# Fewer row dot products inside tile 0's routing, more under the gates, and the gate exponentials ten expert blocks earlier

## The reference

```python
def peer_ffn(h, w_q, sub_k1, sub_k2, expert_u, expert_v):
    q = (ht @ w_q).reshape(T, PEER_HEADS, PEER_QDIM)
    s1 = jnp.einsum('thd,nd->thn', q[..., :PEER_HALF], sub_k1)
    s2 = jnp.einsum('thd,nd->thn', q[..., PEER_HALF:], sub_k2)
    v1, i1 = lax.top_k(s1, PEER_TOPK)
    v2, i2 = lax.top_k(s2, PEER_TOPK)
    cand = v1[..., :, None] + v2[..., None, :]
    vals, pos = lax.top_k(cand.reshape(...), PEER_TOPK)
    experts = jnp.take_along_axis(cand_idx, pos, axis=-1)
    gates = jax.nn.softmax(vals, axis=-1)
    a = jnp.einsum('cd,chkd->chk', xc, expert_u[experts])
    w = jax.nn.gelu(a) * gates
    return jnp.einsum('chk,chkd->cd', w, expert_v[experts])
```

## Time and profile before

| what | value |
|---|---|
| median of 3 runs | 1914.27 us (1913.71 to 1916.34) |
| the profiled execution, its own time | 1914.9 us |
| its span | 1912.9 us |
| mean granted TensorE clock | 0.992 |
| TensorE matmul busy | 1858.3 us, 97% |
| VectorE busy | 790.1 us, 41% |
| ScalarE, GpSimd busy | 259.0 us, 259.7 us |
| chain that ended last | TensorE 78%, DMA 9%, issue 6%, VectorE 5% |
| of it, fetches of v rows, of u rows | 6%, 3% |
| row fetches | 90 u rows and 90 v rows, median 9.2 and 10.0 us from issue to landing |

### The profile page before, as it was taken

How to read it: one execution, slowest core, us unless ns; L and a number is a source line. 1 busy time by engine, 2 the same in 40 slices (tenths; PEclk the granted TensorE clock), 3 DMA queues, 4 the chain that set the end, 5 groups by cost and what they waited for, 6 DMA issues and landing times.

```text
span 1912.9 us, 26633 instructions
## 1 busy us (share of the span) xinstructions
PE 1858.3 (97%) x10710; PEld 1530.9 (80%) x10710; DVE 790.1 (41%) x1739; ACT 259.0 (14%) x601; POOL 259.7 (14%) x252
## 2 busy tenths in 40 slices
PE   7999999999997999999999999999999999999996
PEld 6478575689997999999999957687786968687783
DVE  1410223248795877788644333231123113321122
ACT  1013333013443111000000011110000001110010
POOL 0100000000435333333433100000000000000000
PEclk9999999999998999999999999999999999999998
DMA  6434243244999999899999943364444435344441
GB/s 244 176 132 178 109 148 139 99 165 151 360 408 379 354 345 345 322 362 353 372 417 416 363 163 115 139 222 151 150 152 169 158 110 174 129 160 154 154 152 47
DMA packets 71138, 422.62 MB, mean 221 GB/s; under 512 B 8048, under 2 KB 8048, under 8 KB 31872
## 3 DMA queue, kind: packets, MB, share of 16 engines
q1 hardware_dynamic: 42048, 306.20, 43.6%
q0 software_dynamic: 28272, 111.74, 15.3%
q10 hardware_dynamic: 720, 3.27, 0.4%
HBM read 415.88 MB, written 5.24 MB: 220 GB/s over the span
## 4 chain that ended last, share of the span: by engine, by line
PE 78%; DMA 9%; issue 6%; DVE 5%; ACT 1%; POOL 0%; POOLq 0%; DVEq 0%; ACTq 0%
PE ps L409 23%; PE ps L449 10%; PE ps L752 9%; PE ps L478 7%; PE ps L760 7%; DMA arena<-v_rows,sparse_pairs 6%; PE ps L958 5%; PE ps L418 5%; PE ps L650 3%; DMA arena<-u_rows,sparse_pairs 3%; DVE arena L1555 1%; PE ps L684 1%; PE ps L773 1%; PE ps L546 1%; PE ps L914 1%
## 5 line engine op out<-in xcount | busy, mean ns | idle before, releaser
L409 PE MATMUL ps<-xT,ring 128*128 128x256 f32 x1920 | 420.6, 381 | 2.6 <-DVE xT L1723 2.6
L409 PEld LDWEIGHTS ps<-xT,ring 128*128 128x128 f32 x1920 | 365.7, 191 | 58.2 <-issue 7.0
L752 PE MATMUL ps<-xT,ring 128*128 128x168 f32 x2048 | 299.7, 309 | 0.2 <-ACT arena L1149 0.2
L760 PE MATMUL ps<-arena,ring 128*128 128x168 f32 (+1 forms) x2048 | 297.2, 307 | 0.0
L752 PEld LDWEIGHTS ps<-xT,ring 128*128 128x128 f32 x2048 | 294.5, 192 | 0.5 <-issue 0.5
L760 PEld LDWEIGHTS ps<-arena,ring 128*128 128x128 f32 x2048 | 292.3, 190 | 0.5 <-issue 0.5
L449 PE MATMUL ps<-ring,arena 128*128 128x512 f32 x448 | 196.9, 597 | 3.2 <-DVE arena L1899 2.8
L478 PEld LDWEIGHTS ps<-xT,ring 128*128 128x128 f32 x1536 | 173.4, 192 | 3.0 <-issue 2.9
L478 PE MATMUL ps<-xT,ring 128*128 128x128 f32 x1536 | 174.1, 275 | 0.0
L449 PEld LDWEIGHTS ps<-ring,arena 128*128 128x128 f32 x448 | 84.7, 192 | 104.0 <-issue 99.5
L1917 POOL TENSOR_SCALAR stat<-stat 128x1 f32<-128x1 f32 (+2 forms) x23 | 4.4, 190 | 1016.6 <-DVE stat L1798 759.5
(11 more groups left out here) (245 smaller groups left out, 1394.5 us busy)
## 6 DMA issues: line engine op xcount, KB each, us to landing
ring<-stream SPq DMA_DIRECT2D x292, 1024.0 KB, 5.1
arena<-second_params POOLq DMA_DIRECT2D x6, 1024.0 KB, 5.4
kv_scratch<-arena POOLq DMA_DIRECT2D x4, 1024.0 KB, 8.2
arena<-kv_scratch POOLq DMA_DIRECT2D x2, 2048.0 KB, 11.2
arena<-second_params POOLq DMA_DIRECT2D x1, 1536.0 KB, 6.6
arena<-u_rows,sparse_pairs POOLq DMA_INDIRECT x90, 9.2
arena<-v_rows,sparse_pairs POOLq DMA_INDIRECT x90, 10.0
arena<-mem_T ACTq DMA_DIRECT2D x1, 1024.0 KB, 7.8
```

Of the source, the lines that this page charges most:

```text
L409: ins = pe.matmul(ps[:, bank, t * T:(t + 1) * T], w[:, k * 2 * P + t * P:k * 2 * P + (t + 1) * P], act[:, k, :], start=(k == 0), stop=(k = ...
L752: ins = pe.matmul(ps[:, o % 2, 0:DENSE], w[:, (o % 2) * D + k * P:(o % 2) * D + (k + 1) * P], xT[:, k, 0:DENSE], start=(k == 0), stop=(k = ...
L760: ins = pe.matmul(ps[:, 4 + k // 2, c:c + DENSE], w[:, (o % 2) * D + k * P:(o % 2) * D + (k + 1) * P], H[:, n, :], start=False, stop=last, ...
```

## The change

Five numbers of the hand-written order change. Nothing is computed differently.

- Inside tile 0's routing VectorE does 18 row dots and not 36 (one behind each step of `best16` and not two, and the number at the end of the routing lowered).
- Between the end of the routing and the selector copies it does 16 (18 to 34) and not 10 (36 to 46).
- Under the first half of the gates it does 46 (34 to 80) and not 38 (46 to 84), and the fetch order follows, since U_FIRST is also GpSimd's.
- Under the second half of the gates it does 44 row adds in 21 groups and not 42; so 20 adds, 10 dots and 26 adds are left for the end, 56 in all, where it was 22, 6 and 26, 54 in all.
- ScalarE does the exponentials of tile 0 behind pair 21 (block 42) and not behind pair 26 (block 52).

```diff
@@ -46,10 +46,10 @@
-DOTS_ROUTING = 36
-DOTS_FIRST = 46
+DOTS_ROUTING = 18
+DOTS_FIRST = 34
 ROWS = 5
-U_FIRST = 84
+U_FIRST = 80
@@ -1150,7 +1150,7 @@
-            for i, stop in enumerate((2, 26)):
+            for i, stop in enumerate((2, 21)):
                 with act.Fori(at, stop) as n:
@@ -1610,9 +1610,9 @@
-                    best16(range(16), sc[:, i], top_v, ti, 2)
+                    best16(range(16), sc[:, i], top_v, ti, 1)
                     candidates(range(PH))
-                    best16(range(PH), cand, val, pu, 2)
+                    best16(range(PH), cand, val, pu, 1)
                     shift_gates()
                     pick(i, 0, PH, 2)
                     row_dots(DOTS_ROUTING - dots_done[0])
@@ -1710,7 +1710,7 @@
                     else:
-                        row_adds(2)
+                        row_adds(44 * (g + 1) // GROUPS - adds_done[0])
```

## The result

| what | before | with the change |
|---|---|---|
| median of 5 runs | 1916.34 us (1913.71 to 1918.15) | 1904.73 us (1902.06 to 1907.57) |
| ratio | | 0.9934, 95% interval 0.9922 to 0.9947 |
| profiled execution, span | 1912.9 us | 1900.1 us (its own time 1902.06) |
| mean granted clock | 0.992 | 0.995 |

The change makes the kernel 0.66% faster, 11.6 us in the medians and 12.8 us between the two profiled spans. The predicted 1904.0 us lies 0.7 us from the median. In part that is luck: it was worked out against a median of 1914.27 us, and the kernel before had 1916.34 us beside the changed one; of the 11.6 us won, 10.3 were predicted. In a second series of five runs the changed kernel had 1904.51 us, ratio 0.9940 (0.9926 to 0.9953).

A forecast was written before the change was run, and what follows sets the result against it. TensorE, busy 97% of the span, was taken as the bound, with the row line 4.1 us behind at the fold. Terms: 9.97 + 1.88 - 1.5 = 10.3 us off 1914.27, giving 1904.0 us; range 1901.8 to 1909.6.

The forecast's parts named there:

- The first gap goes: Before tile 0's routing transposes: routing ends at 561.2, 28 us before TensorE asks, so 9.97 us of idle time go.
- The low clock behind it: Blocks 56 to 63, behind the gap: 128 records take 18.45 us and not 20.33, 1.88 us won.
- The exponentials cost nothing: ScalarE, block 42: the exponential and table loads fit into an existing wait for TensorE; `shift_gates` has 16 us of cover.
- The selector copies: L1665, after block 63: done at about 605, needed at 608.8; no cost, cover of 2 to 4 us.
- Under the gates: TensorE's 7.39 us groups: two or three dots or adds fit, 8.3 us of lateness is hidden; no cost on TensorE.
- The end of the row line: Before the fold: 56 rows from 922.5 to 1076.0, TensorE done at 1074.5, so about 1.5 us of waiting given back.
- The sum: Whole kernel: 9.97 + 1.88 - 1.5 = 10.3 us won, so 1904.0 us against 1914.27.
- the upper end of the range: Last 51 rows at 2.9 us instead of 2.81: fold 4.3 us later; with 1.3 us of spread, 1909.6.
- TensorE alone: Rival at the fold: rows come slightly faster, the fold waits for nothing, full 11.85 us won, 1902.4; chance 0.25.
- the first two cases: At the fold: the forecast itself, waiting about 1.5 us for rows (0.62), or no wait and 1902.4 us (0.25).
- the row line could become the bound: Rival at the fold: row line ends at 1087.8, fold waits 13.3 us, 1915.8 or 1917.7; chance 0.04.
- The rival of late copies: Rival after block 63: rows at 4.1 us each, copies done at 627.7, 18.9 us late, 1923.3; chance 0.03.

The follow-up runs named there:

- The run without them: Changed kernel with tile 0's exponentials put back behind pair 26: 1917.05 us, ratio 1.0004.
- The two kernels with 6 dots: Kernel before with DOTS_ROUTING 30, DOTS_FIRST 40: exponentials behind pair 26, 1903.16 us, ratio 0.9929; behind pair 21, 1904.40 us, ratio 0.9941.
- the one-hots' run: Changed kernel with U_FIRST 84, 48 adds, and first one-hots built without waiting for block 63's gelu: 1901.25 us, ratio 0.9919.
- the run with late copies: Changed kernel with DOTS_FIRST 46, so 28 dots and not 16 before the selector copies: 1926.14 us in a single execution.
- the kernel with the rows earlier: Changed kernel with U_FIRST 84 and 48 adds under the gates, 48 rows left for the end: 1903.14 us, ratio 0.9938.
- the kernel with both waits shortened: Changed kernel with U_FIRST 84, 48 adds, one-hots not waiting for block 63's gelu, L409 waiting for single sums: 1902.24 us, again 1898.65 us.

## Why the prediction was right, point by point

- **The first gap goes: right.** 9.97 us are gone. I had L1640 done at 561.2 and tile 0's exponential as what sets it. It starts at 560.64 and ends at 560.93. VectorE waited 1.2 us for the exponential (L1620) there. The margin of 28 us is measured too.
- **The low clock behind it: right, slightly small.** The 128 matmuls take 18.3 to 18.5 us. But I had left the transposes at the 1.12 us that the last four took at the low clock; all eight now take 1.04. TensorE gained 12.6 us until the fold and not 11.85, and this is most of the difference: L792 up to block 56 took 11.69 us and takes 1.04, which is 10.65 and not 9.97.
- **The exponentials cost nothing: right**, and I had underrated them. I treated them as a condition for the gap alone. The run without them shows that their second use is larger: the 16 dots before the copies cannot start earlier than they end, and only the five buffers fill meanwhile.
- **The selector copies: right.** They start at 604.49 and end at 605.4, as expected, 2.5 us before TensorE needs them. But the reason that I gave for 605, some five rows fetched before, did not hold: the first of the 16 dots had its row at hand, the second waited 2.5 us for its own, and they came 2.8 us apart in the mean (560.85 to 603.34). With five at hand the copies would have been done near 599 (an estimate: 561.2 + 5 x 1.145 + 11 x 2.81 + 0.9), so the 605 was partly luck, and 607.1, my bound without them, was reasoned better. The two kernels with 6 dots, late by 1.6 and 4.2 us, lie beyond this edge. It is the nearest cliff of the changed kernel.
- **Under the gates: right.** No new wait of TensorE; the 46 dots and 44 adds are hidden. The two groups with a third add are longer than I had them: an add takes 1.39 us from start to start (five in 6.83 us), so such a group takes 3.69 + 3 x 1.39 = 7.9 us of VectorE and not 7.5. The cover hides that too.
- **The end of the row line: right in kind.** I had it from 922.5 to 1076.0 and a wait of 1.5 us. It ran from 921.58 to 1074.18, and the wait is 0.46 us, 0.41 in the second series. The pace was 2.81 us as before (52 steps from 926.89 to 1072.90). The start came 0.9 us earlier than I had it, mostly for the same 0.7 us of transposes, and the 56 rows took 152.6 us and not 153.5.
- **The sum:** 9.97 + 1.88 - 1.5 = 10.3 against 12.0 us measured at L409. The medians, 11.6 us apart, lie between. (In the upper end of the range, 51 rows at 0.09 us more are 4.6 us and not 4.3.)
- **The rivals.** TensorE alone did not quite end it: the wait of 0.46 us says which of the first two cases it was. The time alone does not, and 11.6 us lie nearer to that rival's 11.85 than to the 10.3 of the forecast. That the row line could become the bound was right as a mechanism; its price was too simple. Ten more rows cost 20 us of waiting and not 28, and the low clock behind a long wait cost 3.3 us in the fold alone, where I had 1.9 for all of it. The rival of late copies was priced at 4.1 us a row; with 28 dots it gave 21 us of wait at a mean of 2.4 us a row (561.1 to 628.2).

What is left open is small for the change itself: 1.1 us of the one-hots' run, and why the executions with six dots and late exponentials differ by up to 10 us, which no single profile places.

## What to carry to other kernels

When work is moved out of the way of one wait, look for the next point at which the same engine is waited for, and for everything that the engine itself waits for in between; here the eighteen dots and the exponentials were worth nothing apart and 12 us together. Move only as much as ends the wait with a margin that you can name: with six dots the time could not be told from that with eighteen, though the copies were then late. A second stream that is just behind the bounding engine, like the rows here, caps what that engine can gain, and its end should be costed with the same care as the gap.

## What the runs showed of the hardware

- A stream that shares the DMA engines speeds up by itself when its neighbour stops: rows came every 2.8 us beside the weight stream and every 1.5 us once TensorE had stood for about 8 us and the stream waited for its ring (the run with late copies: 408 GB/s at 616 to 618 us, 215 at 620 to 622). Some of them had landed by then, and VectorE took those at its own pace.
- The low clock behind a wait costs very different amounts. Behind the 20.5 us wait the fold took 7.02 us and not 3.75. Behind the wait of 2.58 us before L409, the same in all of these kernels, the first 64 matmuls took 15.65 us in the profile of the kernel before and 15.63 in that of the kernel with the rows earlier, and 16.49 and 16.63 in the two profiles of the changed kernel. In the first of these two the clock was low at once:

```profile
1080.00:1082.00 2.00, 1.28 (x3) 1.11 (x4) 0.66 (x2) 0.00 (x0) 0.26 (x1) 0.50 0.81 289
1082.00:1084.00 2.00, 2.00 (x6) 1.55 (x6) 0.00 (x0) 0.00 (x0) 0.00 (x0) 0.50 1.00 418
```

- The same program can have such a stretch in one execution and not in the next. Late in the program TensorE waits 2.81 us before L449, in every kernel here, and 56 matmuls follow. The timelines of the kernel before, of the changed one, and of the two executions of the kernel with both waits shortened (there L451) have them in 26.00 us or in 24.30:

```profile
1562.30 26.00 PE L449 MATMUL ps<-ring,arena 128*128 128x512 f32 x56 [2.81 <-DVE arena L1899]
1551.10 24.30 PE L449 MATMUL ps<-ring,arena 128*128 128x512 f32 x56 [2.81 <-DVE arena L1899]
1547.45 24.30 PE L451 MATMUL ps<-ring,arena 128*128 128x512 f32 x56 [2.81 <-DVE arena L1902]
1546.69 26.00 PE L451 MATMUL ps<-ring,arena 128*128 128x512 f32 x56 [2.81 <-DVE arena L1902]
```

The clock 1 to 2 us behind the start of the first and of the second of these (length, busy PE to POOL, clock, DMA share, GB/s):

```profile
1564.00:1566.00 2.00, 2.00 (x3) 0.79 (x3) 0.00 (x0) 0.00 (x0) 0.00 (x0) 0.50 0.00 0
1552.00:1554.00 2.00, 2.00 (x6) 0.95 (x5) 0.00 (x0) 0.00 (x0) 0.00 (x0) 1.00 0.31 127
```

That is 1.7 us with not one instruction changed. At L411 the same two executions took 16.69 and 15.49 us for the first 64 matmuls behind the same wait of 0.88 us. Differences of 1 to 2 us between single profiles of these kernels can thus be the clock alone and need several runs.
